# Two-block transformer kernel on one core: half-stage scheduling, pieced transfers, and the place of the stick-breaking masks

## The reference, cut to what matters

```python
# block 1, after attention and the recurrent mix
mix = concat([attn, rw]) @ w_out
x = x + rms_norm(mix, norm_mix_post)
u = rms_norm(x, norm_ffn_pre) @ w_ffn_up          # 8192 columns: gate, value
u = conv_b + sum(conv_w[j] * shift(u, 2 - j) for j in range(3))
f = (gelu(gate) * val) @ w_ffn_down
x = x + rms_norm(f, norm_ffn_post)
# block 2: adaptive norm, input product, then among others, per head and block of 128 queries
z = q @ k.T * scale
log_1m_beta = where(s < t, log_sigmoid(-z), 0)
between = reverse_cumsum(log_1m_beta) - log_1m_beta
weights = where(s < t, exp(log_sigmoid(z) + between), 0)
o = weights @ v
```

## Time and profile before

| | |
|---|---|
| median of 3 runs | 2622.97 us (2620.42 to 2623.83) |
| profiled execution, its own time | 2621.15 us |
| its span, first to last instruction | 2619.4 us |
| mean granted TensorE clock | 0.970 |
| busy | TensorE 2471.4 us, VectorE 1191.6, ScalarE 695.3, POOL 919.3 |
| output product and norms of block 1 | about 626 to 766 us of the span |
| feed-forward | about 766 to 1815 us |
| first tiles of block 2 | from about 1815 us |
| stick-breaking part | about 2305 to 2450 us |

### The profile page before, as it was taken

One profiled execution on the slowest core, in us unless ns is written; L12 is line 12 of the kernel. 1 busy time (PEld: TensorE's weight loads), 2 busy tenths in 40 slices (PEclk: granted clock), 3 DMA queues, 4 the chain that ended last, 5 costly groups with the idle time before them and its releaser, 6 DMA issues.

```text
span 2619.4 us, 45567 instructions
## 1 busy us (share of the span) xinstructions
PE 2471.4 (94%) x18246; PEld 1989.7 (76%) x18246; DVE 1191.6 (45%) x1619; ACT 695.3 (27%) x1069; POOL 919.3 (35%) x522
## 2 busy tenths in 40 slices
PE   8999889998989999999999999999999999977797
PEld 6777679985868888888888888877878777733576
DVE  4477776654444422442244223325470666644242
ACT  3233433332332200220022002212352333256421
POOL 3322100012643333333333333365674455400031
PEclk9999989999989999999999999999999999989798
DMA  4211000002322211221122111143321111120021
GB/s 147 74 33 33 25 8 4 5 19 89 113 87 73 73 49 61 73 73 49 59 75 73 50 48 48 48 137 106 133 68 48 46 49 49 58 103 1 1 97 64
DMA packets 47444, 160.24 MB, mean 61 GB/s; under 512 B 4408, under 2 KB 6712, under 8 KB 46904
## 3 DMA queue, kind: packets, MB, share of 16 engines
q1 hardware_dynamic: 27936, 101.72, 12.1%
q10 hardware_dynamic: 19352, 56.31, 6.3%
HBM read 137.57 MB, written 20.45 MB: 60 GB/s over the span
## 4 chain that ended last, share of the span: by engine, by line
PE 83%; DVE 6%; ACT 4%; issue 3%; POOL 2%; DMA 1%; ACTq 0%; DVEq 0%; POOLq 0%; SPq 0%
PE ps L532 52%; PE ps L1098 6%; PE ps L637 5%; PE ps L1121 2%; ACT ab L115 2%; PE ps L801 1%; PE ps L811 1%; PE ps L586 1%; PE ps L808 1%; DVE proj L115 1%; PE ps L542 1%; DVE x_lo L115 1%; POOL w_hi L429 1%; PE ps L1203 1%; POOL w_lo L432 1%
## 5 line engine op out<-in xcount | busy, mean ns | idle before, releaser
L429 POOL TENSOR_TENSOR w_hi<-w_raw,small 128x1024 fp32r<-128x1024 f32 x186 | 359.8, 1935 | 1386.8 <-PE ps L532 1025.2
L532 PE MATMUL ps<-x_hi,w_hi 128*128 128x512 f32 x1600 | 527.3, 395 | 16.7 <-DVE x_lo L115 12.5
L532 PE MATMUL ps<-x_lo,w_hi 128*128 128x512 f32 x1600 | 520.7, 391 | 0.0
L532 PE MATMUL ps<-x_hi,w_lo 128*128 128x512 f32 x1600 | 520.7, 391 | 0.0
L432 POOL TENSOR_TENSOR w_lo<-w_raw,w_hi 128x1024 fp32r<-128x1024 f32 x186 | 455.1, 2447 | 14.6
L532 PEld LDWEIGHTS ps<-x_hi,w_hi 128*128 128x128 f32 x1600 | 301.0, 189 | 89.5 <-DVE x_lo L115 17.8
L532 PEld LDWEIGHTS ps<-x_hi,w_lo 128*128 128x128 f32 x1600 | 302.3, 189 | 63.9
L532 PEld LDWEIGHTS ps<-x_lo,w_hi 128*128 128x128 f32 x1600 | 302.7, 189 | 61.8
L115 DVE SCALAR_TENSOR_TENSOR cv<-ps,cst,cv 128x1023 f32<-128x1023 f32 x64 | 82.1, 1283 | 258.0 <-ACT cv L115 252.6
L532 PE MATMUL ps<-f_hi,w_hi 128*128 128x512 f32 x512 | 170.2, 393 | 3.8 <-POOL w_lo L432 3.8
L532 PE MATMUL ps<-f_lo,w_hi 128*128 128x512 f32 x512 | 168.7, 390 | 0.0
(11 more groups left out here) (298 smaller groups left out, 3834.5 us busy)
## 6 DMA issues: line engine op xcount, KB each, us to landing
w_raw<-wall SPq DMA_DIRECT2D x186, 512.0 KB, 3.5
ada_w<-wada ACTq DMA_DIRECT2D x24, 512.0 KB, 3.5
x_spill<-x ACTq DMA_DIRECT2D x4, 2048.0 KB, 8.9
fill_spill<-stage ACTq DMA_DIRECT2D x24, 256.0 KB, 2.0
x_in<-xT ACTq DMA_DIRECT2D x8, 512.0 KB, 8.4
x<-xT ACTq DMA_DIRECT2D x1, 4096.0 KB, 13.4
x_in<-x_spill ACTq DMA_DIRECT2D x2, 2048.0 KB, 12.7
x<-x_spill ACTq DMA_DIRECT2D x1, 4096.0 KB, 12.5
```

What stands on the lines that cost most here:

```text
L429: nc.gpsimd.tensor_tensor(w_hi[:, u, :, :], w_raw[:, u, :, :], sm["one"].unsqueeze(2).to_broadcast([P, KT, P]), ALU.mult).then_inc(S("w_hi ...
L532: last = mm(ps[:, 2 * u + h, :], w[:, u, k, :], x[:, k, h * 512:(h + 1) * 512], start=(k == 0 and w is w_hi and x is hi), stop=(k == KT - ...
```

## The change

- `x1` is fetched in 8 transfers of 512 KB, `x_again(k)` in front of `mixed(0, k)`.
- `x1_spill(h, k)` stores one tile's half, 256 KB: for half 0 two of them in each of the slots 4 to 7, for half 1 one behind each `scaled_high(1, k)`. The wait before the feed-forward loop counts all 16.
- The last channel tile of the last group is written out. ScalarE's gelu comes in front of the wait for the last up product, the value's scaling, its shifted terms, the product, the high copy and the low part are done in halves, half 0 first.
- The down tiles go in plain order; `down(1, 0)` waits for the second half's low part.
- `x1` comes back in 16 transfers of 256 KB: two in front of each of the first four `ffn_square(0, k)`, then one at the head of each slot `i`, after a wait for the first 8.
- VectorE's `scaled_in(0, k)` runs one tile further ahead in slots 6 and 7 and behind them; for `scaled_up` and for `scaled_in(1, k)` the new loops emit the same order as before, save that `half_pair("a", 1, 1)` comes one tile later.
- In the stick-breaking part `masked(n)` follows `later_keys(n)` and `soft(n + 2)` where the next scores are ahead, and comes in front of `soft(n + 2)` where they are not.

```diff
-    "in_a": ("bias_in", "rmask_in", "x_again", "gmask_in", "sbmask_in"),
+    "in_a": ("bias_in", "rmask_in") + tuple(f"x_again{k}" for k in range(8)) + ("gmask_in", "sbmask_in"),
...
-            down(0, 0, 0, 7)
-            down(0, 1, 0, 7)
-            down(0, 0, 7)
-            down(0, 1, 7)
-            for k in range(2, KT):
+            for k in range(KT):
                 down(0, k)
                 if k in (3, 5, 7):
                     half_sums("a", 2, (k - 3) // 2)
+            pe.wait_ge(S("f_lo_done"), FFN_GROUPS * GROUP + 1)
             down(1, 0, 0, 4)
...
             act.wait_ge(S("x_lo_done"), 16)
-            act.dma_start(x1[:, :, :], dr["xT"].rearrange("p (k t) -> p k t", t=T)).then_inc(landed("x_again")[0], 16)
+
+            def x_again(k):
+                act.dma_start(x1[:, k, :], dr["xT"][:, k * T:(k + 1) * T]).then_inc(landed(f"x_again{k}")[0], 16)
...
             for k in range(KT):
+                x_again(k)
                 mixed(0, k)
...
-                if i == 3:
-                    x1_spill(0)
+                if i >= 4:
+                    x1_spill(0, 2 * i - 8)
+                    x1_spill(0, 2 * i - 7)
...
-            x1_spill(1)
             half_root("b", 1)
             for k in range(KT):
                 scaled_high(1, k)
-            act.wait_ge(S("x1_out"), 32)
+                x1_spill(1, k)
+            act.wait_ge(S("x1_out"), 2 * 16 * KT)
...
-            ffn_up(FFN_GROUPS - 1, False)
+            ffn_up(FFN_GROUPS - 1, False, GROUP - 1)
+
+            def conv_part(u, dst, t):
+                col = 2 * (FFN_GROUPS * GROUP - 1) + u
+                fn(dst[:, t], pair(2 * u)[:, t], ACT.Identity, bias=par("conv_b", col, 1), scale=par("conv_w", 128 + col, 1))\
+                    .then_inc(S("conv_a"), 1)
+
+            act.wait_ge(S("prod"), FFN_GROUPS * GROUP)
+            act.wait_ge(S("gemm_mm"), G_LAST - 1)
+            conv_part(0, cg, slice(0, T))
+            act.wait_ge(S("gemm_evac"), G_LAST - 1)
+            fn(cg[:, :], cg[:, :], ACT.Gelu_apprx_tanh).then_inc(S("gelu"), 1)
+            act.wait_ge(S("gemm_mm"), G_LAST)
+            for h in range(2):
+                conv_part(1, cv, hc(h))
+            for h in range(2):
+                act.wait_ge(S("prod"), FFN_GROUPS * GROUP + 1 + h)
+                copy(f_hi[:, GROUP - 1, hc(h)], gv[:, hc(h)]).then_inc(S("f_hi_done"), 1)
...
             for k in range(KT):
+                if k < KT // 2:
+                    x1_again(0, 2 * k)
+                    x1_again(0, 2 * k + 1)
                 ffn_square(0, k)
             half_root("a", 2)
+            act.wait_ge(S("x1_back"), 16 * KT)
             for i in range(KT):
+                x1_again(1, i)
...
-                    for k in (2, 3, 4):
+                    for k in (2, 3):
                         shifted_high(0, k)
                 ffn_square(1, i)
-            for k in (5, 6, 7):
+            for k in (4, 5, 6, 7):
                 shifted_high(0, k)
...
+            n = 2 * FFN_GROUPS * GROUP
+            dve.wait_ge(S("conv_a"), n - 1)
+            conv_step(0, cg, 0, T, 1)
+            conv_step(0, cg, 0, T, 2).then_inc(S("gemm_evac"), 1)
+            dve.wait_ge(S("conv_a"), n)
+            conv_step(1, cv, 0, 512, 1)
+            conv_step(1, cv, 0, 512, 2)
+            dve.wait_ge(S("gelu"), FFN_GROUPS * GROUP)
+            last_product(0)
+            dve.wait_ge(S("conv_a"), n + 1)
+            conv_step(1, cv, 512, T, 1)
+            last_low(0)
+            conv_step(1, cv, 512, T, 2).then_inc(S("gemm_evac"), 1)
+            last_product(1)
+            last_low(1)
...
                     scaled_in(0, 0)
                     scaled_in(0, 1)
                     shifted_low(0, 0)
+                    scaled_in(0, 2)
                 if i == 7:
-                    for k in (2, 3, 4):
-                        shifted_low(0, k - 1)
-                        scaled_in(0, k)
+                    for k in (1, 2, 3):
+                        shifted_low(0, k)
+                        scaled_in(0, k + 2)
                 add_down(1, i)
...
-            for k in (5, 6, 7):
-                shifted_low(0, k - 1)
-                scaled_in(0, k)
-            shifted_low(0, KT - 1)
+            for k in range(4, KT):
+                shifted_low(0, k)
+                if k + 2 < KT:
+                    scaled_in(0, k + 2)
...
                 for n in (2 * m, 2 * m + 1):
-                    if n:
-                        masked(n - 1)
                     later_keys(n)
-                    if m + 1 < len(SB_STEPS):
+                    if z_ahead(m + 1):
                         soft(n + 2)
-            masked(2 * len(SB_STEPS) - 1)
+                    masked(n)
+                    if m + 1 < len(SB_STEPS) and not z_ahead(m + 1):
+                        soft(n + 2)
```

More of the change, by code:

```diff
@@ L1503, in x1_square, with x1_spill @@
                 half_square("b", h, k, x1[:, k, hc(h)])
[L1505 to L1506 removed]
+            def x1_spill(h, k):
+                act.dma_start(x1_dram.rearrange("p (k t) -> p k t", t=T)[:, k, hc(h)], x1[:, k, hc(h)]).then_inc(S("x1_out"), 16)
             def scaled_high(h, k):
@@ L1532, in _, with ffn_up @@
                 scaled_high(1, k)
-            act.wait_ge(S("x1_out"), 32)
+                x1_spill(1, k)
+            act.wait_ge(S("x1_out"), 2 * 16 * KT)
             eng.preload_act_table_set("gelu_apprx_tanh_and_others")
-            def ffn_up(gr, ada):
-                with act.Fori(0, GROUP) as j:
+            def ffn_up(gr, ada, n=GROUP):
+                with act.Fori(0, n) as j:
                     if ada:
@@ L1560, in _, with x1_again @@
                 ffn_up(gr, True)
-            ffn_up(FFN_GROUPS - 1, False)
+            ffn_up(FFN_GROUPS - 1, False, GROUP - 1)
[14 more added lines that the diff above has]
+                copy(f_hi[:, GROUP - 1, hc(h)], gv[:, hc(h)]).then_inc(S("f_hi_done"), 1)
             eng.preload_act_table_set("sqrt_and_others")
             act.wait_ge(S("gemm_mm"), G_LAST)
-            for h in range(2):
-                act.dma_start(x1_in[h], x1_dram.rearrange("p (k t) -> p k t", t=T)[:, :, hc(h)]).then_inc(S("x1_back"), 16)
+            def x1_again(h, k):
+                act.dma_start(x1_in[h][:, k, :], x1_dram.rearrange("p (k t) -> p k t", t=T)[:, k, hc(h)]).then_inc(S("x1_back"), 16)
             def ffn_square(h, k):
@@ L2137, in _ @@
                 if h == 0:
-                    dve.wait_ge(*landed("x_again"))
+                    dve.wait_ge(*landed(f"x_again{KT - 1}"))
                 dve.wait_ge(S("half_bc_a"), h + 1)
@@ L2150, in _ @@
                     dve.wait_ge(S("res_done"), 2 * KT)
+                scaled_up(h, 0)
                 for k in range(KT):
-                    scaled_up(h, k)
-                    if k:
-                        scaled_low(h, k - 1)
+                    if k < KT - 1:
+                        scaled_up(h, k + 1)
+                    scaled_low(h, k)
                     if h == 0 and k == 3:
                         half_pair("a", 1, 1)
-                scaled_low(h, KT - 1)
                 if h == 0:
@@ L2161, in _, with ffn_up @@
             dve.sem_inc(S("ada_acc"), 1)
-            def ffn_up(gr, ada):
-                with dve.Fori(0, GROUP) as j:
+            def ffn_up(gr, ada, n=GROUP):
+                with dve.Fori(0, n) as j:
                     p = dve.snap(GROUP * gr + j)
@@ L2208, in _, with conv_step, last_product, last_low @@
             ts(sm["ada"][:, 8:16], sm["ada"][:, 8:16], 1.0, None, ALU.add).then_inc(once("ada_done")[0], 1)
-            ffn_up(FFN_GROUPS - 1, False)
+            ffn_up(FFN_GROUPS - 1, False, GROUP - 1)
+            def conv_step(u, dst, lo, hi, back):
+                col = 64 * (2 - back) + 2 * (FFN_GROUPS * GROUP - 1) + u
+                lo = max(lo, back)
+                return stt(dst[:, lo:hi], pair(2 * u)[:, lo - back:hi - back], par("conv_w", col, 1), dst[:, lo:hi],
+                           ALU.mult, ALU.add)
+            def last_product(h):
+                tt(gv[:, hc(h)], cg[:, hc(h)], cv[:, hc(h)], ALU.mult).then_inc(S("prod"), 1)
+            def last_low(h):
+                dve.wait_ge(S("f_hi_done"), FFN_GROUPS * GROUP + h)
+                tt(f_lo[:, GROUP - 1, hc(h)], gv[:, hc(h)], f_hi[:, GROUP - 1, hc(h)].bitcast(F32), ALU.subtract)\
+                    .then_inc(S("f_lo_done"), 1)
+            n = 2 * FFN_GROUPS * GROUP
[13 more added lines that the diff above has]
+            last_low(1)
             def add_down(h, k):
@@ L2238, in _ @@
             half_inverse("a", 2)
-            dve.wait_ge(S("x1_back"), 32)
+            dve.wait_ge(S("x1_back"), 16 * KT)
             for i in range(KT):
@@ L2268, in _ @@
             dve.wait_ge(S("half_bc_a"), 4)
+            dve.wait_ge(S("x1_back"), 2 * 16 * KT)
             for k in range(KT):
@@ L2275, in _ @@
             dve.wait_ge(S("half_bc_b"), 4)
+            scaled_in(1, 0)
             for k in range(KT):
```

(7 more changed lines are left out.)

2 lines of the change are left out of this document (removed).

## The result

The changed kernel took 2604.73 us, median of 5 runs (2600.55 to 2610.39). The kernel before took 2623.83 us beside it (2620.42 to 2627.54, 5 runs). Run again on another occasion it took 2604.42 us against 2620.19, ratio 0.9937 (0.9924 to 0.9949), 16 us. The profiled execution took 2608.97 us, 1.8 more than its span of 2607.2 and 4 above its median. Against the span before (2619.4) it is only 12.2 shorter, so one pair of traces shows less than the medians do.

A forecast was written before the change was run, and what follows sets the result against it. TensorE, busy 94% of the span, was taken as the bound, so only its waits and lower clock count. Terms -0.5 + 0 - 4.7 + 0 - 7.0 - 6.8 = -19.0 gave a median of 2604.0 us, range 2599 to 2612.

The forecast's parts named there:

- all cases but one: The one slower case: issuing a piece holds ScalarE's queue until it lands, together +25.2 us, 2629.2; chance 0.02.
- Pieces of x1: Output product: fetching x1 in 8 transfers removes TensorE's 0.48 us wait for split weights; -0.5 us, between 0 and -0.5.
- Spills: Start of the feed-forward part: the last piece's landing delays the table load, but TensorE does not wait; 0, up to +2.
- Last channel tile: Halves and plain down order start `down(0, 2)` 3.0 us sooner and remove a 1.7 us slow stretch; -4.7, bounds -2.5 to -5.2.
- product 0.69: Last channel tile: VectorE's half-wide product was counted at 0.69 us in the chain to the low part.
- clock term of -1.7: Behind the last channel tile: with no long wait before, 48 products take 11.05 us instead of 12.75; -1.7 us.
- x1 back: Fetching x1 again in 16 transfers: issues fit ScalarE's slots and the last lands well before use; 0, up to +0.6.
- One tile ahead: `head_tile(0, 0)`: tiles come 1.70 us apart instead of 2.35, the clock is kept, the norm's spread comes sooner; -7.0 us.
- the clock is lost at the head tile: Rival for `head_tile(0, 0)`: the clock still falls, so the gain there is only 2.3 us, time 2608.7; chance 0.15.
- Masks: Stick-breaking part: five waits of `weigh` on masked weights, 1.36 or 1.37 us each, go; -6.8 us, between -5.4 and -8.2.
- the mask was not the last wait: Stick-breaking rival: scores or remainders then wait for an exponent or PSUM; half of 6.8 or less remains, 2608 to 2611; chance 0.08.
- more than the sum, because fewer waits lift the clock: Stick-breaking part: with fewer waits, clock dips shrink and 2 to 4 us more come, 2600 to 2602; chance 0.07.

The follow-up runs named there:

- gelu_in_psum: The changed kernel with the last channel tile's gelu written to two free PSUM banks, so its product reads one operand there: 2604.19 us, ratio 0.9937 to the kernel before.
- last_tile_only: The kernel before with only the last channel tile in halves and the down tiles in plain order: 2621.42 us, ratio 0.9997.
- pieces_only: The kernel before with only the three x1 transfers (fetch, spill, return) in pieces: 2621.98 us, ratio 0.9999.
- masks_only: The kernel before with only the new order of the masks in the stick-breaking part: 2618.64 us, ratio 0.9987.
- light_filler: The changed kernel with the last gelu in PSUM and 20 zero products in TensorE's stick-breaking waits: 2595.63 us, ratio 0.9909 to the kernel before.

## Why the prediction was right, and where it was not

The forecast of 2604.0 us met 2604.7 and 2604.4, and the change is faster, as all cases but one said. In each of its places the waits behaved as it said, apart from the 1.97 us for `f_lo`. That the number was met so closely is in part luck: its sum of -19.0 came out once as -19.1 and once as -15.8, and the stages in the traces add to about -12. Point by point:

- **Pieces of x1, -0.5.** Right and a little small: the wait is gone in all 7 traces with pieces. It was 0.5 us in the execution it was read from, but 0.9 to 1.4 in the six others without pieces, and the stage is 1.2 us shorter. The transfer lands in 4.2 us instead of 13.4. In the medians nothing shows.
- **Spills, 0.** Right: no TensorE wait, and the landing is on ScalarE's path and not on TensorE's. The last piece landed in 2.0 us, and the table load waited for it. The changed trace stands 0.59 us later at this place (last copy of a high part at 765.78 for 765.19). Counted from that copy, the table load came at 767.2 on the clock of the old trace (foreseen 767.2 to 767.8) and `cg` at 768.7 (foreseen 769.1), 0.7 us later than before and not 1.1. The 2.0 us for 256 KB are those of the earlier trace rows. The Trainium skill, DMA: Bandwidth & Descriptors, Anatomy of one DMA, gives as an estimate 2.6 us for another issuing path; the measurement decides.
- **Last channel tile, -4.7: the step that was mis-sized, at -2.7** (-3.2 in the profiled pair), near its lower bound of -2.5. The failing term is "product 0.69": it took 2.56 us, and `down(0, 2)` came 1.6 us sooner instead of 3.0. The product read `cg` and `cv` from SBUF while POOL split weights (line 432), and ended 0.55 us behind POOL's end, 1717.23 against 1716.68. The row that 0.69 was taken from, `f_acc<-f_acc,ps` in the earlier trace rows, has an operand in PSUM. gelu_in_psum shows the cause: with one operand in PSUM the product takes 0.69, and 1.6 us come back. The clock term of -1.7 also came only in part: 4 of the 7 traces with a wait of about 2 us had a low stretch behind it.
- **x1 back, 0.** Right: no wait for it shows.
- **One tile ahead, -7.0.** Right against the execution it was worked from (-7.3; pitch 1.69 for 1.70, clock 1.00). But that execution was the worst of five: two others with the old order (last_tile_only, pieces_only) lost less clock there and took 94.56 and 94.30 us for its 97.37. In the mean the part is worth 5.9, and 1.9 us are given back in a low-clock stretch some 60 us later. The rival "the clock is lost at the head tile" fell in all 9 traces. The argument against it was weaker than it looks: the 0.92 in the earlier trace rows covers a stretch whose first 1.0 us is the end of a low one (743.4 to 760.5), so that row shows the clock coming back at the pitch of 1.63 us and not being held.
- **Masks, -6.8: waits right, worth over-stated.** All five waits of 1.36 us are gone, the scores hardly wait longer (12.9 us for 12.4), so the rival "the mask was not the last wait" falls. What failed is that the clock was held fixed. The stretch shrank by 2.4 us in the profiled pair and 4.5 in the mean. gelu_in_psum, whose clock there was 0.91, reached 133.47, a gain of 7.3: the full -6.8 and a little. With the low stretches counted at half their length, the traces give -5.7 in the mean, which is close to masks_only's -5.9 of full-clock time. The case "more than the sum, because fewer waits lift the clock" did not come: the mean clock of the stretch was 0.89 to 0.91 in the five traces with the masks moved and 0.90 to 0.93 in the seven without. The 0.93 of the profiled execution before, from which the term was read, was the best of these seven.

So the sum was close while its terms were too large by some 7 us in the traces. The starting point of 2622.97 was high as well, from 3 runs: over three later groups of 17 to 35 runs the median before was 2620.2 to 2621.9.

## What to carry to other kernels

Price a VectorE instruction that reads two operands from SBUF by what POOL runs at that moment, and put one operand into PSUM where it is on the path. A gain read from a stretch with a low granted clock should be weighed over several executions: such stretches come and go with the same instructions, and removing waits can bring new ones. Zero products in TensorE's waits raised the mean clock (0.97 in the stretch for 0.89), but 49 of them cost more than they gave; try few, and compare by medians of several runs.

## What the runs showed of the hardware

**VectorE behind POOL.** Four instructions with two SBUF operands ended 0.54 to 0.56 us behind the end of the POOL instruction that ran when they started, one that also reads SBUF: 1717.23 behind 1716.68 and 1722.76 behind 1722.22 in the changed kernel, 1717.18 behind 1716.63 and 1720.73 behind 1720.17 in gelu_in_psum. Their lengths were 2.56, 1.60, 0.96 and 1.22 us for the same work of 0.69. The terms of 0.75 us with an operand in PSUM kept their length. It also goes the other way: POOL's split at 1719.94 started 0.16 us behind the second half of `gv` and took 2.28 us, where it takes 1.89 with no such product beside it. The Trainium skill states this (SBUF — State Buffer, section Who interferes with whom): a VectorE instruction with two SBUF inputs contends with a GpSimd one that reads SBUF, and whichever starts later blocks until the other is done. The traces agree in the order of ends; I had not applied it.

**The same instructions, another clock.** An execution spends 123 to 166 us at the lower clock, by the clock that each of the 14 traces records (123 in light_filler, 166 in masks_only). Two executions of the changed kernel differ by 7.0 us in this (145.6 and 152.6), five of kernels with the old head tile by up to 10 us in that stage alone (3.4 to 13.7). That is the size of the effects this change is made of.
